# Projections of heads 1 to 7 of a two-layer mLSTM / Conformer step as three products of split operands

## What is computed

```python
def mlstm_mixer(h, w_in, w_conv, b_gate, gn_g, w_out, C0, n0, m0):
    proj = h @ w_in
    qk = proj[..., :2 * A_QK]
    v = proj[..., 2 * A_QK:2 * A_QK + A_VW]
    o = proj[..., 2 * A_QK + A_VW:2 * A_QK + 2 * A_VW]
    g = proj[..., 2 * A_QK + 2 * A_VW:]
    qk = jax.nn.silu(dwconv(qk, w_conv))
    ...
    hf, (Cf, nf, mf) = mlstm_chunkwise(q, k, vh, i_f, logf_f, C0[:, 0], n0[:, 0], m0[:, 0])
    hb, (Cb, nb, mb) = mlstm_chunkwise(flip(q), flip(k), flip(vh), flip(i_b), flip(logf_b),
                                       C0[:, 1], n0[:, 1], m0[:, 1])
    hs = hf + flip(hb)
    hs = hs * lax.rsqrt(jnp.mean(hs * hs, axis=-1, keepdims=True) + EPS)
    hs = hs.transpose(0, 2, 1, 3).reshape(B, L, A_VW).astype(h.dtype) * gn_g
    out = (jax.nn.sigmoid(o) * hs) @ w_out
```

## Time and profile before

| what | value |
|---|---|
| median of 3 runs | 1906.11 us (1902.64 to 1907.49) |
| the profiled execution, its own time | 1906.12 us |
| its span, first to last instruction | 1904.4 us |
| busy: PE, DVE, ACT, POOL | 1801.2, 1416.2, 1070.5, 48.1 us |
| mixer, head 0 to head 7's projections | about 49 to 273 us of the span |
| HBM traffic | 298 GB/s over the span |

### The profile page before, as it was taken

One profiled execution on the slowest core, in us unless ns is written; L12 is line 12 of the kernel. 1 busy time (PEld: TensorE's weight loads), 2 busy tenths in 40 slices (PEclk: granted clock), 3 DMA queues, 4 the chain that ended last, 5 costly groups with the idle time before them and its releaser, 6 DMA issues.

```text
span 1904.4 us, 24867 instructions
## 1 busy us (share of the span) xinstructions
PE 1801.2 (95%) x8964; PEld 1484.9 (78%) x8964; DVE 1416.2 (74%) x1568; ACT 1070.5 (56%) x1067; POOL 48.1 (3%) x95
## 2 busy tenths in 40 slices
PE   6999999799999998599999999999999999999993
PEld 3778876799997875488888888888888888888883
DVE  1544435565655783499999999999999999999995
ACT  1222224433343222377777777777777777777772
POOL 0001100000000000100000000000000000000001
PEclk8999999899999999599999999999999999999997
DMA  9466678354545653399999999999999999999972
GB/s 391 159 250 230 220 260 320 126 197 172 196 174 207 261 210 132 110 381 379 381 377 376 377 380 381 376 381 374 379 381 378 378 380 377 377 377 372 384 297 88
DMA packets 63002, 568.57 MB, mean 299 GB/s; under 512 B 7268, under 2 KB 7396, under 8 KB 15204
## 3 DMA queue, kind: packets, MB, share of 16 engines
q1 hardware_dynamic: 54144, 539.13, 73.3%
q0 software_dynamic: 5392, 19.41, 2.8%
q10 hardware_dynamic: 3412, 9.28, 1.2%
HBM read 549.43 MB, written 18.36 MB: 298 GB/s over the span
## 4 chain that ended last, share of the span: by engine, by line
PE 88%; DVE 4%; DMA 3%; issue 2%; ACT 2%; POOL 0%; DVEq 0%; POOLq 0%; SPq 0%; ACTq 0%
PE ps L1531 22%; PE ps L1533 22%; PE ps L1532 22%; PE ps L1396 6%; PE ps L1623 3%; PE ps L1393 3%; DMA ring<-mix 2%; PE ps L1318 2%; PE ps L1524 1%; PE ps L1613 1%; PE ps L1707 1%; DVE w_lo L1279 1%; ACT w_hi L840 1%; PE ps L1449 1%; PE ps L1419 1%
## 5 line engine op out<-in xcount | busy, mean ns | idle before, releaser
L1279 DVE TENSOR_TENSOR w_lo<-ring,w_hi 128x1536 fp32r<-128x1536 f32 x504 | 873.8, 1756 | 76.4 <-ACT w_hi L840 76.0
L840 ACT ACTIVATE w_hi<-ring 128x1536 fp32r<-128x1536 f32 x504 | 751.0, 1492 | 232.3 <-PE ps L1533 221.9
L1531 PE MATMUL ps<-w_hi,hg 128*128 128x512 f32 x1072 | 424.8, 396 | 6.7 <-DVE w_lo L1279 4.4
L1532 PE MATMUL ps<-w_lo,hg 128*128 128x512 f32 x1072 | 419.5, 391 | 0.0
L1533 PE MATMUL ps<-w_hi,hg 128*128 128x512 f32 x1008 | 393.6, 390 | 0.0
L1533 PE MATMUL ps<-w_hi,hid 128*128 128x512 f32 x680 | 265.8, 391 | 0.0
L1531 PE MATMUL ps<-w_hi,hid 128*128 128x512 f32 x616 | 241.9, 393 | 3.1 <-DVE hid L1273 3.1
L1532 PE MATMUL ps<-w_lo,hid 128*128 128x512 f32 x616 | 240.0, 390 | 0.0
L1531 PEld LDWEIGHTS ps<-w_hi,hg 128*128 128x128 f32 x1072 | 202.5, 189 | 47.6 <-DVE w_lo L1279 4.8
L1532 PEld LDWEIGHTS ps<-w_lo,hg 128*128 128x128 f32 x1072 | 202.8, 189 | 40.8
L1533 PEld LDWEIGHTS ps<-w_hi,hg 128*128 128x128 f32 x1008 | 189.7, 188 | 40.2
(11 more groups left out here) (235 smaller groups left out, 1670.9 us busy)
## 6 DMA issues: line engine op xcount, KB each, us to landing
ring<-moe SPq DMA_DIRECT2D x252, 1536.0 KB, 8.3
ring<-mix SPq DMA_DIRECT2D x92, 1024.0 KB, 6.9
ring<-ff SPq DMA_DIRECT2D x28, 1536.0 KB, 6.5
xg<-work POOLq DMA_DIRECT2D x12, 512.0 KB, 6.5
so<-xg POOLq DMA_DIRECT2D x10, 512.0 KB, 8.8
yg<-so ACTq DMA_DIRECT2D x10, 512.0 KB, 9.2
work<-c POOLq DMA_DIRECT2D x8, 257.0 KB, 7.1
c_out<-work ACTq DMA_DIRECT2D x8, 257.0 KB, 6.0
```

The costliest lines, as they stand in the source:

```text
L840: act.activation(w_hi[:, s % W_BUFS, :], ring[:, sl, s % 2 * CUT * ROW:(s % 2 + 1) * CUT * ROW], ACT.Copy).then_inc(hi_ready, 1)
L1279: TT(w_lo[:, s % W_BUFS, :], ring[:, slot(ST_MOE + s // 2), s % 2 * CUT * ROW:(s % 2 + 1) * CUT * ROW], w_hi[:, s % W_BUFS, :].bitcast(f32 ...
L1531: pe.matmul(out, a_hi, b_hi, start=start, stop=False)
L1532: pe.matmul(out, a_hi, b_lo, start=False, stop=False)
```

## The change

Head 0 stays as it was. The other 21 projections (`IN_PLAIN` = 3) are done by `project_split`. The activations are split once, after the first norm: ACT copies `hT` to float32r in two halves, DVE subtracts. Each weight stage is split in two halves of 128x1024, numbered n: `in_high(n)` on ACT, `in_low(n)` on DVE, in three buffers. The copies lie in the idle columns of the ring's slots (a second name for the same memory, `ring_r`), the remainders in `hid` and `hT_lo`, which the mixer doesn't use otherwise. ACT reuses a buffer when PE is through with half n - 3 (`in_used` for a first half, `stage_used` for a second). PE does each half as 4 x 2 groups of `three`, 48 matmuls for a projection in place of 16. The copy of v out of PSUM moves ahead of the square of the head in ACT's stream.

```diff
+        plain = ExitStack()
+        ring = plain.enter_context(nc.sbuf_tensor("ring", [P, SLOTS, STAGE], f32))
+        plain.close()
+        ring_r = ctx.enter_context(nc.sbuf_tensor("ring_r", [P, SLOTS, STAGE], mybir.dt.float32r))
...
+        in_hT_hi, in_hT_lo, in_w_hi = ([ring_r[:, b, MIX:STAGE].rearrange("p (k t) -> p k t", t=T) for b in blocks]
+                                       for blocks in ((0, 1), (2, 3), (4, 5, 6)))
...
+            for b in range(2):
+                act.wait_ge(hT0_ready, 4 * b + 4)
+                act.wait_ge(hT1_ready, 4 * b + 4)
+                act.activation(in_hT_hi[b], hT[:, 4 * b:4 * b + 4, :], ACT.Copy).then_inc(in_hT_hi_ready, 1)
+
+            def in_high(n):
+                stage, cols = in_half(n)
+                act.wait_ge(loaded[slot(stage)], 16 * (stage // SLOTS + 1))
+                if n >= IN_BUFS:
+                    before, _ = in_half(n - IN_BUFS)
+                    if (n - IN_BUFS) % 2 == 0:
+                        act.wait_ge(in_used, (n - IN_BUFS) // 2 + 1)
+                    else:
+                        act.wait_ge(stage_used, before + 1)
+                act.activation(in_w_hi[n % IN_BUFS], ring[:, slot(stage), cols].rearrange("p (k t) -> p k t", t=T),
+                               ACT.Copy).then_inc(in_high_ready, 1)
...
             decay_scores(0)
+            in_high(0)
+            in_high(1)
             for h in range(HEADS):
...
                 decay_scores(it + 1)
                 if more_in:
+                    in_high(n + 2)
+                    in_high(n + 3)
                     qk_out(h + 1)
+                    in_high(n + 4)
...
                     qk_tanh(h + 1)
+                    in_high(n + 5)
+                    v_out(h + 1)
                 head_squared(it)
                 if more_in:
-                    v_out(h + 1)
                     decay_scores(it + 1)
+                    if h + 2 < HEADS:
+                        in_high(n + 6)
                     o_out(h + 1)
+                    if h + 2 < HEADS:
+                        in_high(n + 7)
...
+            def in_low(n):
+                stage, cols = in_half(n)
+                dve.wait_ge(in_high_ready, n + 1)
+                TT(in_w_lo[n % IN_BUFS], ring[:, slot(stage), cols].rearrange("p (k t) -> p k t", t=T),
+                   in_w_hi[n % IN_BUFS].bitcast(f32), ALU.subtract).then_inc(in_split, 1)
...
                 head_normed(it)
+                if more_in:
+                    in_low(n + 2)
+                    in_low(n + 3)
                 if h >= 1:
                     modulations(it - 1)
                 if more_in:
                     conv_qk(h + 1)
                 out_gate(it)
+                if more_in:
+                    in_low(n + 4)
...
                 head_sum(it)
                 if more_in:
+                    in_low(n + 5)
                     masked(it + 1)
                     weighted_keys(it + 1)
                     weighted(it + 1)
                     head_normed(it)
+                    if h + 2 < HEADS:
+                        in_low(n + 6)
                     o_gate(h + 1)
+                    if h + 2 < HEADS:
+                        in_low(n + 7)
...
+            def project_split(s):
+                pe.wait_ge(proj_out, s)
+                if s == IN_PLAIN:
+                    pe.wait_ge(in_hT_lo_ready, 2)
+                for i in range(2):
+                    n = 2 * (s - IN_PLAIN) + i
+                    pe.wait_ge(in_split, n + 1)
+                    t_hi, t_lo, w_h, w_l = in_hT_hi[i], in_hT_lo[i], in_w_hi[n % IN_BUFS], in_w_lo[n % IN_BUFS]
+                    for j in range(2):
+                        out, half = ps[:, MISC, j * T:(j + 1) * T], slice(j * P, (j + 1) * P)
+                        for k in range(4):
+                            begin, end = (i, j, k) == (0, 0, 0), (i, j, k) == (1, 1, 3)
+                            if s % 3 == 1:
+                                ins = three(out, t_hi[:, k, half], t_lo[:, k, half], w_h[:, k, :], w_l[:, k, :], begin, end)
+                            else:
+                                ins = three(out, w_h[:, k, half], w_l[:, k, half], t_hi[:, k, :], t_lo[:, k, :], begin, end)
+                    ins.then_inc(stage_used if i else in_used, 1)
...
             def project(s):
 
+                if s >= IN_PLAIN:
+                    project_split(s)
+                    return
```

More of the change, by code:

```diff
@@ L42 @@
 N_IN = 3 * HEADS
+IN_PLAIN = 3
+IN_BUFS = 3
 ADA_LAST = 2 * KD
@@ L178, in sem @@
             return ctx.enter_context(nc.semaphore(name))
-        ring = sb("ring", P, SLOTS, STAGE)
+        plain = ExitStack()
+        ring = plain.enter_context(nc.sbuf_tensor("ring", [P, SLOTS, STAGE], f32))
+        plain.close()
+        ring_r = ctx.enter_context(nc.sbuf_tensor("ring_r", [P, SLOTS, STAGE], mybir.dt.float32r))
         x = sb("x", P, G, D)
@@ L315, in mlstm_conformer_kernel @@
         hid_hi, hid_lo = hid[:, 0:2, :], hid[:, 2:4, :]
+        hT_lo_end = part("hT_lo", P, KD // 2, T)
+        in_hT_hi, in_hT_lo, in_w_hi = ([ring_r[:, b, MIX:STAGE].rearrange("p (k t) -> p k t", t=T) for b in blocks]
+                                       for blocks in ((0, 1), (2, 3), (4, 5, 6)))
+        in_w_lo = [hid[:, 2 * b:2 * b + 2, :].rearrange("p a (k t) -> p (a k) t", t=T) for b in range(2)]
+        in_w_lo.append(hT_lo_end[:, :, :])
         hT_hi = hg[:, :, :, :].rearrange("p a k t -> p (a k t)").rearrange("p (k t) -> p k t", t=T)
-        hT_lo = [hid[:, 2:4, :].rearrange("p a (k t) -> p (a k) t", t=T), part("hT_lo", P, KD // 2, T)[:, :, :]]
+        hT_lo = [hid[:, 2:4, :].rearrange("p a (k t) -> p (a k) t", t=T), hT_lo_end[:, :, :]]
         og_hi, og_lo = (a.rearrange(n).rearrange("p (s c t) -> p s c t", s=4, c=2)
@@ L338, in mlstm_conformer_kernel @@
         mod_ready, ada_out, ada_turned = sem("mod_ready"), sem("ada_out"), sem("ada_turned")
+        in_hT_hi_ready, in_hT_lo_ready = sem("in_hT_hi_ready"), sem("in_hT_lo_ready")
+        in_high_ready, in_split, in_used = sem("in_high_ready"), sem("in_split"), sem("in_used")
         gates_tok, gates_out = sem("gates_tok"), sem("gates_out")
@@ L396, in wide_done, with in_half @@
             return [a // KD - 1 for a in range(before + 1, after + 1) if a % KD == 0]
+        def in_half(n):
+            return IN_STAGE[IN_PLAIN + n // 2], slice(n % 2 * (MIX // 2), (n % 2 + 1) * (MIX // 2))
         @block.sync
@@ L670, in _ @@
             decay_scores(0)
+            in_high(0)
+            in_high(1)
             for h in range(HEADS):
                 more_in = h + 1 < HEADS
+                n = 6 * h
                 it = 2 * h
@@ L923, in _ @@
             norm_turn(0)
+            for b in range(2):
+                dve.wait_ge(in_hT_hi_ready, b + 1)
+                TT(in_hT_lo[b], hT[:, 4 * b:4 * b + 4, :], in_hT_hi[b].bitcast(f32), ALU.subtract
+                   ).then_inc(in_hT_lo_ready, 1)
+            def in_low(n):
[3 more added lines that the diff above has]
+                   in_w_hi[n % IN_BUFS].bitcast(f32), ALU.subtract).then_inc(in_split, 1)
             dve.wait_ge(gate_raw, 2)
@@ L1060, in _ @@
             weighted(0)
+            in_low(0)
+            in_low(1)
             for h in range(HEADS):
                 more_in = h + 1 < HEADS
+                n = 6 * h
                 it = 2 * h
@@ L1380, in gates_turn, with three @@
                 ins.then_inc(gates_psum, 1)
+            def three(out, a_hi, a_lo, b_hi, b_lo, start, stop):
+                pe.matmul(out, a_hi, b_hi, start=start, stop=False)
+                pe.matmul(out, a_hi, b_lo, start=False, stop=False)
+                return pe.matmul(out, a_lo, b_hi, start=False, stop=stop)
+            def project_split(s):
[15 more added lines that the diff above has]
+                    ins.then_inc(stage_used if i else in_used, 1)
             def project(s):
+                if s >= IN_PLAIN:
+                    project_split(s)
+                    return
                 w = arrived(IN_STAGE[s])
@@ L1527, in down @@
                     ins.then_inc(stage_used, 1)
[L1529 to L1533, removed]
             pe.wait_ge(og_ready, ITS)
```

## The result

The changed kernel took 1888.04 us (median of 4 runs, 1886.48 to 1891.10), the kernel before, on the same chip, 1906.80 us: a ratio of 0.9905 (0.9890 to 0.9921). The forecast was 1885.5 us with 1879 to 1893 around it. The profiled execution took 1886.48 us, with a span of 1884.7 us; that of before had 1904.4.

A forecast was written before the change was run, and what follows sets the result against it. The prediction took PE to bound the mixer: 1906.12 us less 24.2 for 21 projections plus 3.6 for six border waits gave 1885.5 us, with a range of 1879 to 1893.

The forecast's parts named there:

- PE bounds the mixer, nothing else changes behind it: Mixer: PE alone sets the pace, 29.10 us a head; everything behind it moves forward as it stands.
- The wait of 1.42 us for a load at the mixer's end: Mixer's end: PE's wait for a load at 291.65 us stays, the loads being issued behind head 7's o projection.
- 1.15 us a projection, from the FFN's 0.120 us a product: Projections: 48 products at 0.120 us take 5.76 us in place of 6.91; 21 projections save 24.2 us.
- its further 0.19 us at the entry: qk projection's entry behind the front step: the extra 0.19 us stay; if they went, 1.3 us more saved.
- products could stream at 0.108 us: Rival, projections: products stream without a step for the weights, 5.18 us a projection, total 1873.4 us; chance 0.04.
- the rival of splits that serialise the head: Rival, mixer: DVE and ACT never work at once, a head takes 32.8 us, seven heads give 1932 us; chance 0.03.
- 0.6 us at each of six borders: Border of two heads: front step waits for out_gate behind the last split, 0.4 to 0.9 us each, 3.6 us in all.
- No wait in the odd iteration, margin 1.0 us: Odd iteration: silu ends 7.5 us after qk, PE asks at 8.55, so the subtraction ahead of silu costs nothing.
- The splits of `hT`, the first and middle splits, the loads: Mixer: splits fall in idle time or beside qk, loads reach some 265 GB/s below 430; no cost.
- The value copy costs nothing and saves nothing: ACT's stream: moving v's copy ahead of the square holds nothing up and saves nothing where PE doesn't wait.
- The clock costs nothing: PE's clock: border waits of 0.6 us in 26 are unlike the pause before the half level; cost nothing.
- The noise: Measurement: three runs of before lie 5 us apart, which a median feels by 1 or 2 us.

The follow-up runs named there:

- the change again: The change rerun unedited for further profiles: 1883.52 us (median of 5 runs), 0.9874 of the kernel before, and 1887.90 us in one run.
- the kernel with plain products: Against the change: all splits made and waited for, but PE does the projections with 16 float32 matmuls again; 1912.73 us, 1.0019 of the kernel before.
- the mended kernel: Against the change: a head's last subtraction, in_low(n+7), moved behind the next head's out_gate; 1884.11 and 1884.39 us on two chips.
- the tripled subtraction: Against the change: in_low(n+4), the subtraction ahead of silu in the odd iteration, made three times; 1896.18 us in one run.

## Why the prediction was right, point by point

The forecast lay 2.5 us below the measured median, within its range. The profiles say how near the sum itself was: from head 0's `o_out` to the `ada` stage behind the last projection before takes 208.7 us (64.14 to 272.86) and the change 188.1 (64.69 to 252.79). That is 20.6 us, the whole sum. Ahead of it the change was 0.55 us later and behind it 0.4 us longer, which gives the 19.7 of the span. The steps:

- *PE bounds the mixer, nothing else changes behind it.* Right in sum: 1631.9 us from the last `ada` stage behind a projection to the end, before 1631.5. The parts of it move, with the clock's spells and with waits for loads, as they do from one execution to the next: up to the convolution's first projection 344.2 us in the change and 346.8 in the change again, 345.2 and 347.5 in the two profiles of before. The wait of 1.42 us for a load at the mixer's end, which was to stay, was 0.63 in the change.
- *1.15 us a projection, from the FFN's 0.120 us a product.* Right: 0.120 us, and 1.16 from the kernel with plain products, qk among them, so its further 0.19 us at the entry stayed. That products could stream at 0.108 us fell with it. So did the rival of splits that serialise the head: DVE and ACT together are busy for 31.8 us in a head of 26.25.
- *0.6 us at each of six borders.* Right: 0.64 by the mended kernel. From the `ada` stage behind head 1's qk projection to the one behind head 7's o, 20 projections: 20 x 1.15 - 6 x 0.6 = 19.4 us, and 193.65 - 174.07 = 19.6 us were measured. A head was to be 26.25 us, and is.
- *No wait in the odd iteration, margin 1.0 us.* Right: 1.3 in the timeline, 1.2 by the tripled subtraction.
- *The splits of `hT`, the first and middle splits, the loads.* Nothing of these shows as a wait of PE; the loads reach 261 GB/s in a head. That is 6.9 MB a head, as 235 GB/s over 29.10 us is: the 5 MB in my text was wrong, and the rates, which the step went by, were not.
- *The value copy costs nothing and saves nothing.* The step that failed. Set against the new order I had looked at what the copy holds up, not at what would hold up the copy. The same walk had the numbers: the head's sum ends 9.7 us after qk, so the square and a copy behind it (1.2 us in the profile) end after 10.9, and the o projection starts at 9.9. It is worth 0.91 us a head, 5.7 us in all, near a third of the result. The sum was not touched by it, since the kernel as changed has no wait there; the total came out right in spite of this step and not by it. A forecast of a version without the move would have been wrong by 5.7 us.
- *The clock costs nothing.* Right for the borders: no wait of 0.40 us was followed by the half level. Open behind the mixer, where the convolution's first projection took 8.83 us in every profile with the products.
- *The noise.* I gave a median 1 or 2 us. Two sessions gave the change 18.8 and 24.6 us below the kernel before; the clock's spells are worth about 3 us at head 1's qk and 1.7 us at the convolution's first projection, and a median of five doesn't average them out. That may also be why the mended border, 3.8 us in the profile, gave 1884.39 against 1883.52 for the change in one session: no difference that these runs can tell. The numbers of it rest on the profiled heads, and on another chip on the 9.9 us between it and the kernel with the value copy behind, of which it is 3.8 in the profiles' 9.5.

The kernel with the border mended beats the kernel before clearly (0.9857 and 0.9874 in two sessions), and the change by 0.64 us a border in its profile, which the medians neither show nor exclude.

## What to carry to other kernels

When PE is shortened and the work moves to engines that work in order, walk each added instruction against the moment at which PE asks for what stands behind it: of the two places where a subtraction was made longer, one had 1.2 us to spare, and the other, behind the last product of a head, had none, and its wait gave back 0.64 us of the head's 3.45. Look at a move in another stream from both sides, what it holds up and what would hold it up: the cheap-looking one was worth near a third of the gain. And an idle gap in the profile is less than its price, 0.40 us shown and 0.64 paid: take the price from start to start against a kernel without the wait.

## What the runs showed of the hardware

The price of a wait on PE is larger than its gap by 0.24 to 0.28 us: at a float32 matmul behind a wait (0.40 shown and 0.64 paid at the border; 1.00 shown and 1.28 paid in the odd iteration with the tripled subtraction) and at a product behind one (0.63 shown, 0.91 paid). At the border 0.17 of it is the overlap of two records that a start without a wait has (0.86 us from start to start, a record of 1.03), and 0.07 a slower first pair of matmuls (0.39 us in place of 0.32). Whether that last part is the weight load, which otherwise lies beside the matmul before, wasn't tested.

A product of 128x128 by 128x256 in float32r with a weight load of its own starts every 0.120 us at full clock, in the projections as in the FFN; a float32 matmul of the same shape takes 0.432 us (16 in 6.91), so the three products cost 0.83 of it.

The half clock behind one and the same pause of 1.8 us lasts about 4 us in one execution of a kernel and some 10 in the next, for the kernel before and the changed one alike.
